# LayerNorm gamma and beta applied to the transposed copy, as per-partition scalars, while it leaves PSUM

## The reference

```python
h = layer_norm(concat([meta, x]), ln_in_g, ln_in_b)
mix = hybrid_mixer(h, w_in, b_in, ...)       # sliding-window attention || gated linear attention, then w_out
h = layer_norm(ALPHA*h + mix, ln1_g, ln1_b)
h = layer_norm(ALPHA*h + swiglu(h, w_ffn_gate, w_ffn_up, w_ffn_down), ln2_g, ln2_b)
# layer_norm: (x - mu) * rsqrt(var + eps) * g + b, over the 1024 features
```

## Time and profile before

| | |
|---|---|
| median of 2 runs | 3241.91 us (3238.35 to 3245.48) |
| profiled execution | 3242.24 us |
| its span, slowest core (2) | 3240.5 us |
| cores | 3207.5 to 3240.5 us, granted clock 0.820 to 0.835 |
| PE busy | 2229.3 us (69%) |
| DVE busy | 1200.3 us (37%) |
| ACT busy | 887.5 us (27%) |
| POOL busy | 510.7 us (16%) |

### The profile page before, as it was taken

The page is one execution under the profiler, slowest core; times in us unless marked ns, Lnnn a source line. Parts: engine busy times, 40 slices in busy tenths (PEclk is TensorE's granted clock), DMA queues, the critical chain, the costliest instruction groups (busy, mean ns, idle before and its releaser), DMA issues.

```text
span 3240.5 us, 35774 instructions; the slowest of 8 cores (3207.5 to 3240.5 us)
## 1 busy us (share of the span) xinstructions
PE 2229.3 (69%) x11766; PEld 1136.3 (35%) x11766; DVE 1200.3 (37%) x1944; ACT 887.5 (27%) x1574; POOL 510.7 (16%) x345
## 2 busy tenths in 40 slices
PE   0131666887488866987489875887488865987585
PEld 0020343443344343444344342443344342443331
DVE  0120225234542345234542246334542355234532
ACT  0120223322332233322332233323232233323211
POOL 0033302010310112010310113010310112010301
PEclk9965668997699876887699877997699877997797
DMA  7077602210131102220131102220131102211042
GB/s 134 26 75 71 82 1 86 78 62 30 46 117 62 56 20 94 69 66 33 46 117 60 58 7 106 77 63 29 46 117 63 56 21 103 73 58 40 35 131 88
DMA packets 120547, 210.85 MB, mean 65 GB/s; under 512 B 55944, under 2 KB 62105, under 8 KB 120367
## 3 DMA queue, kind: packets, MB, share of 16 engines
q1 hardware_dynamic: 61938, 167.64, 15.9%
q0 software_dynamic: 58432, 40.93, 7.7%
HBM read 215.91 MB, written 34.08 MB: 77 GB/s over the span
## 4 chain that ended last, share of the span: by engine, by line
PE 53%; DVE 13%; ACT 9%; issue 9%; DMA 8%; POOL 6%; DVEq 1%; ACTq 0%; SPq 0%; POOLq 0%
PE PB L437 30%; PE PB L766 10%; DMA wgu_s<-w_ffn_gate 4%; POOL H L805 3%; PE PB L629 2%; DMA BCOL<-b_in 2%; DVE LST L783 1%; ACT L450 1%; ACT GB L644 1%; POOL AT L805 1%; DVE LST L782 1%; DVE OGT L650 1%; DVE SGF L752 1%; PE PB L452 1%; PE PB L730 1%
## 5 line engine op out<-in xcount | busy, mean ns | idle before, releaser
L437 PE MATMUL PB<-HT,WGU 128*128 128x512 bf16 x2816 | 675.6, 398 | 69.7 <-DVE SGF L752 40.5
L437 PEld LDWEIGHTS PB<-HT,WGU 128*128 128x128 bf16 x2816 | 278.4, 102 | 445.3 <-issue 191.1
L437 PE MATMUL PB<-HT,W_IN 128*64 128x128 bf16 (+3 forms) x3776 | 397.2, 277 | 21.6 <-DVE OST L735 20.3
L766 PE MATMUL PB<-WD,AT 128*128 128x512 bf16 x1408 | 374.6, 414 | 23.6 <-DVE H L773 13.9
L437 PEld LDWEIGHTS PB<-HT,W_IN 128*64 128x64 bf16 (+2 forms) x3776 | 306.1, 123 | 135.1 <-issue 60.3
L805 POOL TENSOR_TENSOR H<-H,LNC 128x1024 f32<-128x1024 f32 x64 | 179.6, 2820 | 795.4 <-DVE H L802 795.1
L703 POOL TENSOR_TENSOR PT<-PT,MCUR 128x512 bf16<-128x512 bf16 x64 | 74.2, 1159 | 1249.6 <-ACT PT L702 1249.5
L752 DVE SCALAR_TENSOR_TENSOR SGF<-SGF,PB 128x512 f32<-128x512 f32 x176 | 121.0, 688 | 380.1 <-ACT SGF L751 375.4
L421 PE MATMUL PB<-IDENT,H 128*128 128x128 f32 x256 | 61.2, 420 | 236.4 <-POOL H L805 235.8
L766 PEld LDWEIGHTS PB<-WD,AT 128*128 128x128 bf16 x1408 | 136.5, 105 | 233.5 <-issue 122.1
L734 DVE RECIPROCAL RDEN<-PB 128x256 f32<-128x256 f32 x64 | 112.5, 1758 | 240.5 <-PE PB L730 240.5
(11 more groups left out here) (145 smaller groups left out, 2698.4 us busy)
## 6 DMA issues: line engine op xcount, KB each, us to landing
WGU<-wgu_s SPq DMA_DIRECT2D x176, 512.0 KB, 3.5
WD<-wd_s SPq DMA_DIRECT2D x176, 256.0 KB, 2.6
XS<-x SPq DMA_DIRECT2D x32, 512.0 KB, 4.4
out<-H POOLq DMA_DIRECT2D x32, 512.0 KB, 2.9
AT<-x SPq DMA_DIRECT2D x16, 512.0 KB, 4.8
wgu_s<-w_ffn_gate POOLq DMA_DIRECT2D x22, 256.0 KB, 5.5
wgu_s<-w_ffn_up POOLq DMA_DIRECT2D x22, 256.0 KB, 4.6
wd_s<-w_ffn_down POOLq DMA_DIRECT2D x22, 256.0 KB, 7.0
```

The costliest lines, as they stand in the source:

```text
L437: i = e.matmul(out_ap, lhsT=l, rhs=r, start=(idx == 0), stop=(idx == n - 1))
L766: i = e.matmul(PB[4 + j][:, :], lhsT=AT[:, fc, j * 128:(j + 1) * 128], rhs=WD[wb][:, sub, :], start=(fc == 0), stop=(fc == NFC - 1))
```

## The change

Six things change. (1) A new tile `LNCOL` holds the gammas and betas of the input LayerNorm and LayerNorm 1 as columns, feature kk*128+p in partition p; it is filled by 32 single-column DMAs on SP, which are marked as writing `BCOL`, between ACT's scaling of `BCOL` and the load of `SINK32`. (2) `transpose_tile` has an argument `gcol`; with it, each half leaves PSUM in four 128x128 instructions, which multiply by a gamma column and add a beta column, on ACT for the first half and on DVE for the second. (3) `ln_in_tile` only normalises. (4) Tiles 2 and 3 get gamma (DVE) and beta (POOL) after their transposes, since `XS` is their residual; tiles 0 and 1 don't. (5) In `tails`, the transposes stand right behind the normalisation; the same four gamma products and four beta additions on `H` follow them. (6) The meta tile is as before.

```diff
+        for vi, base in ((0, 0), (1, 8), (2, 16), (3, 24)):
+            for kk in range(8):
+                P.dma("sp", LNCOL[:, base + kk:base + kk + 1], lnv[vi][kk * 128:(kk + 1) * 128].rearrange("(p o) -> p o", o=1),
+                      writes=bl("BCOL"))
         P.dma("sp", SINK32[32:33, :], sinks.rearrange("(o n) -> o n", o=1), writes=bl("SINK32"))
...
-            layer_norm_apply(xs[:, :], xs[:, :], 128, 0, xb, xb, L, lb)
+            P.op("act", lambda e: e.activation(out=xs[:, :], in_=xs[:, :], func=AF.Identity, bias=L[:, 15:16], scale=L[:, 14:15]),
+                 reads=xb + lb, writes=xb)
...
+        def ln_in_affine(xs, xb):
+            P.op("dve", lambda e: e.tensor_tensor(out=xs[:, :], in0=xs[:, :], in1=LNC[:, 0, :], op=ALU.mult), reads=xb + bl("LNC"), writes=xb)
+            P.op("pool", lambda e: e.tensor_tensor(out=xs[:, :], in0=xs[:, :], in1=LNC[:, 1, :], op=ALU.add), reads=xb + bl("LNC"), writes=xb)
...
+                if gcol is not None:
+                    for k in range(4):
+                        kk = half * 4 + k
+                        dst1 = HTd[:, kk, j * 128:(j + 1) * 128]
+                        ps1 = PB[pb][:, k * 128:(k + 1) * 128]
+                        gA = LNCOL[:, gcol + kk:gcol + kk + 1]
+                        bA = LNCOL[:, gcol + 8 + kk:gcol + 9 + kk]
+                        if eng == "act":
+                            P.op("act", lambda e, ...: e.activation(out=dst1, in_=ps1, func=AF.Identity, bias=bA, scale=gA),
+                                 reads=bl(f"PB{pb}", "BCOL"), writes=dstb)
+                        else:
+                            P.op("dve", lambda e, ...: e.tensor_scalar(out=dst1, in0=ps1, scalar1=gA, scalar2=bA, op0=ALU.mult, op1=ALU.add),
+                                 reads=bl(f"PB{pb}", "BCOL"), writes=dstb)
+                    continue
...
                 xs, xb = ln_in_tile(T)
+                yield 6.0
+                transpose_tile(xs, xb, HT0, bl(f"HT0_{j}"), j, (0, 1), gcol=0)
+                if j >= 2 or debug:
+                    ln_in_affine(xs, xb)
...
             for (t, tb, gi), (L, lb) in zip(items, stats):
                 ln_n(t, tb, L, lb)
+            for j in range(4):
+                transpose_tile(H[:, j, :], bl(f"H{j}"), HT1, bl(f"HT1_{j}"), j, (2 * j, 2 * j + 1), gcol=16)
             for (t, tb, gi) in items:
                 ln_g(t, tb, gi)
...
-                transpose_tile(H[:, j, :], bl(f"H{j}"), HT1, bl(f"HT1_{j}"), j, (2 * j, 2 * j + 1))
```

More of the change, by code:

```diff
@@ L242, in _build @@
         NEGH = sb("NEGH", [128, 1], F32)
+        LNCOL = sb("LNCOL", [128, 32], F32)
         SINK32 = sb("SINK32", [33, 8], F32)
@@ L411, in ln_in_tile, with transpose_tile @@
             L, lb = layer_norm_stats(xs[:, :], 128, xb)
-            layer_norm_apply(xs[:, :], xs[:, :], 128, 0, xb, xb, L, lb)
+            P.op("act", lambda e: e.activation(out=xs[:, :], in_=xs[:, :], func=AF.Identity, bias=L[:, 15:16], scale=L[:, 14:15]),
+                 reads=xb + lb, writes=xb)
             return xs, xb
-        def transpose_tile(src, srcb, HTd, dstb, j, banks):
+        def ln_in_affine(xs, xb):
+            P.op("dve", lambda e: e.tensor_tensor(out=xs[:, :], in0=xs[:, :], in1=LNC[:, 0, :], op=ALU.mult), reads=xb + bl("LNC"), writes=xb)
+            P.op("pool", lambda e: e.tensor_tensor(out=xs[:, :], in0=xs[:, :], in1=LNC[:, 1, :], op=ALU.add), reads=xb + bl("LNC"), writes=xb)
+        def transpose_tile(src, srcb, HTd, dstb, j, banks, gcol=None):
             for half, eng in ((0, "act"), (1, "dve")):
@@ L424, in transpose_tile @@
                 P.op("pe", tr, reads=srcb + bl("CONST"), writes=bl(f"PB{pb}"))
+                if gcol is not None:
[6 more added lines that the diff above has]
+                        if eng == "act":
+                            P.op("act", lambda e, dst1=dst1, ps1=ps1, gA=gA, bA=bA: e.activation(out=dst1, in_=ps1, func=AF.Identity, bias=bA, scale=gA),
+                                 reads=bl(f"PB{pb}", "BCOL"), writes=dstb)
+                        else:
+                            P.op("dve", lambda e, dst1=dst1, ps1=ps1, gA=gA, bA=bA: e.tensor_scalar(out=dst1, in0=ps1, scalar1=gA, scalar2=bA,
+                                                                                                   op0=ALU.mult, op1=ALU.add),
+                                 reads=bl(f"PB{pb}", "BCOL"), writes=dstb)
+                    continue
                 dst = HTd[:, half * 4:(half + 1) * 4, j * 128:(j + 1) * 128]
@@ L529, in mixer_head @@
                 xs, xb = ln_in_tile(T)
+                yield 6.0
+                transpose_tile(xs, xb, HT0, bl(f"HT0_{j}"), j, (0, 1), gcol=0)
+                if j >= 2 or debug:
+                    ln_in_affine(xs, xb)
                 if debug:
                     P.dma("pool", dbg_h0[T * 128:(T + 1) * 128, :], xs[:, :], reads=xb)
-                yield 6.0
-                transpose_tile(xs, xb, HT0, bl(f"HT0_{j}"), j, (0, 1))
                 yield 1.5
```

## The result

The changed kernel is slower. The ratio to the kernel before is **1.058**, 95% interval 1.055 to 1.062: some 3430 us against 3242 us. The profiled execution took 3430.85 us; its slowest core, 2, spans 3429.3 us against 3240.5. That is 189 us more where I had forecast 143, and it lies above my range (3310 to 3415).

What follows compares the result with a forecast made beforehand. The prediction saw PE held by short serial chains and a start where PE hardly works. Its terms, 52 + 6 x 14 + 8 - 1 = +143 us on 3242.2, gave 3385 us, range 3310 to 3415.

Steps and rivals of the forecast that it cites:

- The clock: FFN's beginning: after PE idles some 7 us at the third fc, its matmuls run slower, +1.5 us a block.
- The mixer's tiles: Between the FFN's third fc and the projections: narrow evacuations and tile 2's moved product lengthen PE's waits, +6.2 us a block.
- The start: Before the first attention mask: 32 serial column loads, later POOL casts and idling at tile 2, +52 us (bounds 38 and 66).
- The tail: Tails and FFN's beginning: FFN starts 2.5 us earlier, but products delay the third fc; +6 for seven blocks, last tail -1.
- The rest: One of seven blocks, slowed by a lower granted clock, hides more: +8 us there instead of 14.
- (A): Rival, evacuations: narrow instructions pipeline 0.26 us apart, a block costs about 5 us instead of 14; 3325 us, chance 0.17.
- (B): Rival, tails and FFN: slower DVE work is covered, the start alone counts, less 2.5 a tail; 3274 us, chance 0.10.
- (C): Rival, start: column loads overlap and cost nothing, the rest stands; 3321 us, chance 0.06.
- (D): Rival, tail: faster, last evacuation follows the norms at once, products covered, start's price gone; 3150 us, chance of faster 0.03.

Runs made afterwards that it cites:

- e5: Changed kernel with unneeded matmuls into an unused PSUM bank where PE would wait: some 3372 us, ratio 1.042 to the kernel before.
- e6: Changed kernel with a tracked buffer of its own for each 128x128 piece of HT0 and HT1, column loads still serial: 3279.42 us, ratio 1.014.
- e11: Changed kernel with overlapping loads, own buffers per piece, half of tile 0's tail copies moved to DVE, products and additions on H and tiles 2, 3 later: 3161.08 us, 0.979.
- e9: Kernel before with overlapping loads and the changed tail, shared buffers kept, gamma products and beta additions on H behind fc 14 to 20: 3209.95 us, ratio 0.994.
- e2: Changed kernel with each of the 32 columns a buffer of its own, loaded behind SINK32 so that loads overlap: 3369.42 us, ratio 1.042.
- e4: Kernel before with overlapping column loads and the changed tail only, mixer's tiles as before: 3284.35 us, ratio 1.016.

## Why the prediction was wrong, step by step

The direction was right, and so were the mechanisms. Against the slowest core the forecast was 46 us short (51 against the median core), and the step that failed is one term of the sum.

**The clock (failed).** The term was mis-sized: +1.5 us a block, measured 6.9. I had written "After 3.22 us of idling, 16 matmuls took 5.01 us where others took 3.61" and added 1.5 for it, once a block. PE's busy time between the third fc and the projections grew by **6.9** us a block: 7 x 5.4 = 38 us of the 51. I had lengthened three more waits in the same forecast (tile 1, tile 2, tile 3) and priced none of them with it; I kept that for the upper end of the range ("the clock is lost at two more waits of a block"). The rows after show four such places: +2.8 (behind the third fc's wait, where I had 1.5), +2.65, +1.7 and +1.5 us, 8.6 in all, less the 1.4 that the earlier trace rows already had. e5 takes just this away, and 51 us with it. The range's upper end was too low by its own terms, too: 3385 + 14 for the start and 21 for two more waits of 1.5 in seven blocks is 3420, not 3415; the measured 3430 lies above both.

**The mixer's tiles.** Forecast +6.2 a block of waiting, measured +7.5: 9 us in all. Of the evacuation's prices, those within a tile were right: 0.55 us from one ACT piece to the next. The second pointer on DVE, for which I took no surcharge, costs 0.06 (410 ns against 351), the upper bound that I had named.

**The start.** Forecast +52, measured +48 by the cores' medians. On core 2 the mask came 60 us later, not 52. Its casts start 2 us later than I had them and the idle time at tile 2 is 6.3 us, not 13.7, but the pairs before it are slower (waits of 7.00 and 9.44 us for a landing, where the first ones before had been 4.46 and 5.61). Why they are is open; the start differs by 19 us between cores in any case.

**The tail.** The FFN starts 3.1 us earlier a tail (forecast 2.5): I had all sixteen pieces of ACT 0.55 apart, but the first of a tile, which writes another buffer, starts 0.36 behind the last of the tile before, and the sixteen take 8.09 us, not 8.8. From there to the third fc it takes 9.0 us more (forecast 8.5). In it is a thing that I hadn't seen: the `VS` copy, 2.1 us longer. That the sum came out so near is in part luck: without the copy my 8.5 would have been 1.6 too high. Both together are -25 + 65 = +40, where I had 6 x 7 - 1 = +41.

**The rest.** I had taken 6 us off for the one block that ran at a lower granted clock. Core 2's rest, where that block had stood, fell by 13 us; the median core's rose by 5. On core 2, then, the terms are +65, -25, +65, +58 and +39 (idle and busy time of seven blocks) and -13, together 189. My own terms in that order were +52, and +41 for the two of the tail, then +43, +10.5 and -4: the clock is 28 of the 46 us missing there, the mixer's waits 15 and the start 13, and the rest takes 9 back.

**The rivals.** (A), the narrow instructions pipeline, is false for the kernel as written, and true once they write separate buffers: then they start 0.35 apart (not 0.26), and e6 came to 3279. My argument, that `L644` with its one buffer was the nearest row, was the right one. By the page "VectorE: DVE Perf Modes" of the Trainium skill, section "The TRN2 errata", they would last 0.26 and 0.25 us (my estimates); the rows have 410 and 456 ns, and the shortest mean of any run here is 402 (e11, DVE) and 455 (e9, ACT). (B), DVE's work is covered, is false: 9.32 us of wait. It becomes nearly true by moving that work, which is e9 (7 us left of 65). (C), the column loads overlap, is false as written, and true with separate buffers; it is worth 61 us by the cores' medians, where I had 64. (D), faster, with 3150 for a tail whose copies follow the norms at once, covered products and a start at no price: e11, which is nearest to that, took 3161. That the two are so close is partly luck: e11's tails gain 8.5 us each, not 10, and its start 23 us, not 12, while tiles of the mixer still cost 11.

## What to carry to other kernels

A wait that a change lengthens on the matrix engine can cost its own length and then the clock, as the waits of 4.40, 5.41 and 9.32 us did here: look in the trace for the same matmuls behind a short and a long wait, and charge the difference at every place where the wait grows, not once. When one instruction is cut into several, ask first what tracks their output: here the shared buffer made strung copies and serial loads out of work that overlaps. Own buffers gave some 150 us at the copies (e6) and some 60 at the loads (e2); moving the tail's products gave some 75 (e4 to e9). And work taken off a chain isn't free where it is put down; in the tail it cost 65 us ahead of the instruction for which the next stage waits, and nothing visible behind the fifteenth of 22 steps.

## What the runs showed of the hardware that I had not expected

- A bfloat16 copy of 128x128 on DVE, SBUF to SBUF, took 184 ns in all seven blocks before, and 2327 ns on the average beside a POOL addition of 128x1024 float32. In every kernel with those additions at that place it was 2.3 or 2.4 us (2.33, 2.34, 2.37), and 0.18 or 0.19 in the others. And in each of the seven blocks it ended 0.05 us behind the end of a POOL addition, in all five kernels that have the slow copy. Here it is the copy of 977.13 to 979.45:

```profile
976.09 3.32 POOL L832 TENSOR_TENSOR H<-H,LNC 128x1024 f32<-128x1024 f32 x1
```

- The Trainium skill's page "SBUF — State Buffer", section "SBUF: two separate sides", says that VectorE and GpSimd share one pair of ports, which only some of VectorE's instructions need, and that whichever instruction starts first holds it until it ends, while the other is blocked. The copy's end agrees with that: it comes 0.05 us behind the end of POOL's addition in all seven blocks. That this copy is one of the instructions that need the pair, no run here shows.
- ACT's pieces that write one tracked buffer started 0.55 us apart, and 0.35 where each wrote its own; each lasted 0.46 in both cases, so without the wait they overlap. On DVE it was 0.52 and 0.32, at 0.41.
- Eight single-column loads were issued in 3.65 us, 0.46 each, when none waited for another, and in 16.3 when each did.
